# Gate and up projections that move the high and low halves of the activations in one matmul, with squares folded on VectorE and masks added in place

## What is computed

```python
x = x + 0.5 * swiglu(rmsnorm(x, g1), w_gate, w_up, w_down)      # F = 2816
h = rmsnorm(x, g_mix)
o = gla_attention(...)  or  mla_attention(...)                   # layer 0, layer 1
x = x + concat([o, memory_cross_attention(...)]) @ w_out
x = x + 0.5 * swiglu(rmsnorm(x, g2), w_gate2, w_up2, w_down2)

def swiglu(h, w_gate, w_up, w_down):
    return (silu(h @ w_gate) * (h @ w_up)) @ w_down
```

## Time and profile before

| | us |
|---|---|
| median of 3 executions (1849.73 to 1852.27) | 1849.98 |
| profiled execution, its own time | 1849.6 |
| its span in the profile | 1847.8 |
| TensorE busy | 1731.1 |
| VectorE busy | 1185.5 |
| ScalarE busy | 906.3 |
| GpSimd busy | 146.6 |
| DMA traffic, mean | 156 GB/s |
| granted TensorE clock, mean share of full speed | 0.971 |

### The profile page before, as it was taken

The page is one execution under the profiler, slowest core; times in us unless marked ns, Lnnn a source line. Parts: engine busy times, 40 slices in busy tenths (PEclk is TensorE's granted clock), DMA queues, the critical chain, the costliest instruction groups (busy, mean ns, idle before and its releaser), DMA issues.

```text
span 1847.8 us, 33177 instructions
## 1 busy us (share of the span) xinstructions
PE 1731.1 (94%) x12716; PEld 1619.7 (88%) x12716; DVE 1185.5 (64%) x1681; ACT 906.3 (49%) x1462; POOL 146.6 (8%) x125
## 2 busy tenths in 40 slices
PE   7999999899999999999799999997899988989997
PEld 7999987599999999987589999874899977689997
DVE  5756676456656676677656765657666568666554
ACT  5544453544444454445545544546554445655443
POOL 1100300001000200032102000300100003010000
PEclk9999999999999999999899999999899999999998
DMA  6555444245655465545134655440365544036552
GB/s 234 198 184 183 145 150 161 67 160 172 200 185 174 135 217 184 178 160 182 46 125 149 204 180 183 157 140 12 103 218 182 187 140 137 16 111 217 189 183 70
DMA packets 79333, 287.34 MB, mean 156 GB/s; under 512 B 8848, under 2 KB 9232, under 8 KB 79008
## 3 DMA queue, kind: packets, MB, share of 16 engines
q1 hardware_dynamic: 78336, 282.25, 46.0%
q0 software_dynamic: 608, 3.15, 0.5%
q10 hardware_dynamic: 320, 1.01, 0.2%
HBM read 285.31 MB, written 1.05 MB: 155 GB/s over the span
## 4 chain that ended last, share of the span: by engine, by line
PE 68%; issue 12%; DVE 10%; ACT 4%; POOL 3%; DMA 2%; POOLq 0%; ACTq 0%; SPq 0%; DVEq 0%
PE ps L1779 10%; PE ps L1780 10%; PE ps L1781 10%; PE ps L1718 8%; PE ps L1765 7%; PE ps L1767 7%; PE ps L1766 7%; DMA raw<-units 2%; POOL rows L570 2%; DVE act_lo L1098 2%; PE ps L2060 1%; DVE wlo L1064 1%; PE ps L2024 1%; DVE inv L1580 1%; ACT prob L1007 1%
## 5 line engine op out<-in xcount | busy, mean ns | idle before, releaser
L1239 DVE TENSOR_TENSOR wlo<-raw,whi 128x1024 fp32r<-128x1024 f32 x380 | 464.2, 1225 | 256.2 <-ACT whi L838 255.3
L1779 PE MATMUL ps<-act_hi,wlo 128*128 128x256 f32 x2016 | 575.2, 285 | 4.2 <-DVE prob L1247 4.2
L1781 PE MATMUL ps<-act_lo,whi 128*128 128x256 f32 x2016 | 573.3, 284 | 0.0
L1780 PE MATMUL ps<-act_hi,whi 128*128 128x256 f32 x2016 | 573.2, 284 | 0.0
L838 ACT ACTIVATE whi<-raw 128x1024 fp32r<-128x1024 f32 x380 | 397.8, 1049 | 169.4 <-PE ps L1781 120.9
L1779 PEld LDWEIGHTS ps<-act_hi,wlo 128*128 128x128 f32 x2016 | 390.0, 193 | 4.8 <-issue 4.6
L1780 PEld LDWEIGHTS ps<-act_hi,whi 128*128 128x128 f32 x2016 | 389.9, 193 | 0.2
L1781 PEld LDWEIGHTS ps<-act_lo,whi 128*128 128x128 f32 x2016 | 389.8, 193 | 0.0
L1765 PE MATMUL ps<-hid_hi,wlo 128*128 128x256 f32 x1056 | 298.8, 283 | 0.0
L1766 PE MATMUL ps<-hid_hi,whi 128*128 128x256 f32 x1056 | 298.8, 283 | 0.0
L1767 PE MATMUL ps<-hid_lo,whi 128*128 128x256 f32 x1056 | 298.8, 283 | 0.0
(11 more groups left out here) (208 smaller groups left out, 2123.9 us busy)
## 6 DMA issues: line engine op xcount, KB each, us to landing
raw<-units SPq DMA_DIRECT2D x534, 512.0 KB, 3.4
arena<-mem_in POOLq DMA_DIRECT2D x2, 1024.0 KB, 8.0
x<-x_in SPq DMA_DIRECT2D x4, 256.0 KB, 5.0
arena<-mem_in POOLq DMA_DIRECT2D x4, 256.0 KB, 4.6
out<-x SPq DMA_DIRECT2D x4, 256.0 KB, 2.3
const<-const_in ACTq DMA_DIRECT2D x1, 816.0 KB, 6.7
row<-row_in ACTq DMA_DIRECT2D x1, 134.0 KB, 6.6
gain<-gain_in SPq DMA_DIRECT2D x1, 76.5 KB, 2.0
```

Of the source, the lines that this page charges most:

```text
L1239: V.tensor_tensor(wlo[:, u % RING, :], raw[:, u % RAW, :], whi[:, u % RING, :].bitcast(F32), ALU.subtract).then_inc(lo_ready, 1)
L1779: T.matmul(out_, wlo[:, slot, w], act_hi[:, k, :], start=k == 0, stop=False)
L1780: T.matmul(out_, whi[:, slot, w], act_hi[:, k, :], start=False, stop=False)
L1781: ins = T.matmul(out_, whi[:, slot, w], act_lo[:, k, :], start=False, stop=k == KD - 1)
```

## The change

1. `act_hi` and `act_lo` become the two halves of one tile, `acts[:, k, 0]` and `acts[:, k, 1]`. In `columns`, `whi` is loaded once per k and moves both halves, 512 columns, into a whole bank; `wlo` moves the high half, 256 columns, into the bank's first half. Gate and up of a chunk lie in two banks (4 and 5, or 6 and 7), and chunks alternate between the pairs as before.
2. On evacuation ScalarE copies the two banks' second halves to SBUF (`lows_out`, a new instruction per chunk), VectorE adds the first halves (`added_up`, new), then multiplies by the inverse norm from SBUF to SBUF. gate(c) waits for `added_up` of chunk c-2. In the first chunk of a stage VectorE's mean, diagonal and copy of the spread now stand behind that add; before, they stood ahead of chunk 0 and waited for no chunk.
3. The four squares of x are folded on VectorE, right after the low parts of the activations and ahead of the next two unit splits. GpSimd keeps the folding of the memory tokens' squares.
4. The masks hold the 256 columns in which anything is masked, and are added in place in PSUM. For causal jobs the two token tiles' scores change places in the bank, so that those columns are contiguous. The wait for the transposes of job j-4 goes. The constants shrink from 1632 to 1120 columns beside the identity.
5. For sink heads the two small VectorE steps become one, with a negated sink prepared once, and ScalarE's two sink exponentials of a job become one.

The core of the diff:

```diff
+        acts = sb("acts", [P, 16, 2, S], F32R)
+        act_hi, act_lo = acts[:, :, 0, :], acts[:, :, 1, :]
...
@@ ScalarE, chunk
+                        act.wait_ge(unit_used, i * RING + (U0 + (2 * (c + 1) if c < 3 else 3 * c)))
+                        nc.scalar.activation(gate_up_rms[:, c % 2], ps[:, bank:bank + 2, S:2 * S], ACT.Copy
+                                             ).then_inc(lows_out, 1)
...
@@ VectorE, norm and norm_beside_memory
-                    self.squares += BANKS
+                    self.folded()
...
@@ VectorE, chunk
-                        V.tensor_tensor(gate_up_rms[:, c % 2], ps[:, bank, :].rearrange("p (e s) -> p e s", e=2),
-                                        doubled(inv_rms), ALU.mult).then_inc(scaled_ready, 1)
+                        dve.wait_ge(lows_out, i * 2 + n)
+                        V.tensor_tensor(both, ps[:, bank:bank + 2, 0:S], both, ALU.add).then_inc(added_up, 1)
+                        if c == 0:
+                            self.mean(name, 0)
...
+                            self.diagonal(name)
+                            self.spread(0)
+                            dve.wait_ge(inv_ready, self.spreads)
+                        dve.wait_ge(added_up, i * 2 + n)
+                        V.tensor_tensor(both, both, doubled(inv_rms), ALU.mult).then_inc(scaled_ready, 1)
...
@@ VectorE, attention
+                                middle = ps[:, j % NB, P:3 * P]
+                                self.step(V.tensor_tensor(middle, middle, job["mask"], ALU.add))
...
-                                self.step(V.tensor_scalar(inv[:, j % NB, :], inv[:, j % NB, :], HD ** -0.5, job["sink"],
-                                                          ALU.mult, ALU.max))
-                                V.tensor_scalar(top[:, j % NB, :], inv[:, j % NB, :], -1.0, None,
-                                                ALU.mult).then_inc(top_ready, 1)
+                                V.tensor_scalar(top[:, j % NB, :], inv[:, j % NB, :], -HD ** -0.5, job["minus_sink"],
+                                                ALU.mult, ALU.min).then_inc(top_ready, 1)
...
@@ TensorE, columns
-                            T.matmul(out_, wlo[:, slot, w], act_hi[:, k, :], start=k == 0, stop=False)
-                            T.matmul(out_, whi[:, slot, w], act_hi[:, k, :], start=False, stop=False)
-                            ins = T.matmul(out_, whi[:, slot, w], act_lo[:, k, :], start=False, stop=k == KD - 1)
+                            T.matmul(ps[:, bank, :], whi[:, slot, w], acts[:, k].rearrange("p e s -> p (e s)"),
+                                     start=k == 0, stop=False)
+                            ins = T.matmul(ps[:, bank, 0:S], wlo[:, slot, w], act_hi[:, k, :], start=False,
+                                           stop=k == KD - 1)
...
@@ TensorE, gate; the feed-forward stage's order
+                        if c >= 2:
+                            pe.wait_ge(added_up, i * 2 + (gu + c - 1))
...
-                    self.columns_of_fold(0, 5)
+                    self.columns_of_fold(0, 0)
...
-                    self.spread(5)
+                    self.spread(0)
...
+                    pe.wait_ge(inv_ready, self.diags)
                     down(0, 0, first=True)
-                    pe.wait_ge(inv_ready, self.diags)
```

More of the change, by code:

```diff
@@ L318, in build @@
         rstd = sb("rstd", [P, STAT_W])
+        minus_sink = sb("minus_sink", [P, QH])
         minus_half = sb("minus_half", [P, 32])
@@ L495, in keys_of, with scores_of @@
             return (t + 1) * P if job["causal"] else S
+        def scores_of(job, j, t):
+            at = S * (1 - t if job["causal"] else t)
+            return ps[:, j % NB, at:at + keys_of(job, t)]
         def queries_of(job, k):
@@ L1000, in attention @@
                                 n_keys = keys_of(job, t)
[L1001 to L1005 removed]
+                                if job["sink"] is not None and t == 0:
+                                    nc.scalar.activation(es[:, j % NB, :], top[:, j % NB, :], ACT.Exp, bias=job["sink"])
+                                src = scores_of(job, j, t)
                                 scale = HD ** -0.5 if job["rms"] is None else query_scale(job)[:, t:t + 1]
@@ L1100, in low, with folded @@
                                            ).then_inc(norm_lo, 1)
+                def folded(self):
+                    for b in range(1, BANKS):
+                        dve.wait_ge(square_ready, self.squares + b + 1)
+                        self.step(V.tensor_tensor(sq[:, 0], sq[:, 0], sq[:, b], ALU.add))
+                    self.squares += BANKS
+                    V.tensor_tensor(fold[:, 0, :], sq[:, 0, 0:S], sq[:, 0, S:2 * S], ALU.add).then_inc(fold_ready, 1)
                 def mean(self, name, bank):
@@ L1290, in end @@
                     if end.startswith(("post", "fpost")):
-                        for b in range(1, BANKS):
-                            dve.wait_ge(square_ready, self.squares + b + 1)
-                            self.step(V.tensor_tensor(sq[:, 0], sq[:, 0], sq[:, b], ALU.add))
-                        self.squares += BANKS
-                        V.tensor_tensor(fold[:, 0, :], sq[:, 0, 0:S], sq[:, 0, S:2 * S], ALU.add
-                                        ).then_inc(fold_ready, 1)
+                        self.folded()
                         self.mean(end, 5)
@@ L1320, in gla @@
                     dve.wait_ge(params_landed, 48)
+                    V.tensor_scalar(minus_sink[:], row[:, ROW_AT["sink"]:ROW_AT["sink"] + QH], -1.0, None, ALU.mult)
                     self.norm_memory_keys(0)
```

86 lines of the change are left out of this document (32 added, 54 removed).

## The result

The changed kernel takes **1819.1 us** in the median (1817.2 to 1820.5, four runs), the kernel before beside it 1850.4 (1849.7 to 1852.3): a ratio of 0.983, with a 95% interval of 0.982 to 0.985. It is 31 us faster where 37 were forecast, inside the range, 6 us short of the forecast. The profiled execution took 1819.4 us, its span 1817.6.

The account below looks back on a forecast made before the run. TensorE, busy 94% of the span, was taken as the bound in the gate and up projections. Terms of 21.5 + 8 + 1 + 0.5 + 6 = 37.0 us off 1849.6 gave 1812.6, forecast as a 1813 us median; range 1804 to 1830.

Parts of the forecast that it names:

- Two matmuls for three: Gate and up projections (`columns`): one matmul fewer per k saves 11 ns, 2016 times less the first stage's loss, 21.5 us.
- I take 0.349, nearer to the end whose sum is explained: In `columns`, a 512 and a 256 per k cost 0.349 us, chosen from 0.347 to 0.354.
- Rival (a): In `columns`, a 256 beside a 512 costs more on top, so a k saves perhaps 2.5 ns: 1829 us; 10%.
- rival (c): In `columns`, a 512 ahead of a shorter matmul costs 0.254, a k 0.374: slower, 1862 us; 3%.
- (d): In `columns`, TensorE takes the 512 as two parts, so the pair gains nothing: 1834 us; 2%.
- The longer evacuation: Feed-forward chunks: ScalarE's new copy and VectorE's new add are covered by TensorE's work; 0, up to 2 us of loss.
- The fold: Stage starts: folding on VectorE removes TensorE's waits for GpSimd, 8 us, plus 1 us in the last stage.
- three stages give 1.5 each: Starts of three feed-forward stages: the vanished wait and faster low parts gain 1.5 us each, 4.5 together.
- The fifth stage: nothing: Fifth stage's start: no gain from faster low parts, since TensorE itself is slow there at the lower clock.
- The first stage's start: First stage's loads: a later diagonal loses about 1 us, smaller constants save 1.6 us of traffic; 0.5 us gained.
- Masks and sinks: Attention: cheaper mask add and one small step fewer give 5.5 us in banded jobs, 0.5 in causal: 6 us.
- Rival (b): Fold, evacuation and masks: the small parts don't come, some 4 of 15.5 us stay: 1824 us; 20%.

Follow-up runs that it names:

- The later memory steps: The changed kernel with ScalarE's and VectorE's two memory-token steps placed later in three feed-forward stages: 1811.6 us, ratio 0.980 to the kernel before.

## Why the prediction was nearly right, point by point

**1. Two matmuls for three: mechanism right, term mis-sized.** 21.5 us forecast, 14 measured. The step that failed is "I take 0.349, nearer to the end whose sum is explained". The sum of rows 5 and 6 put a 512 and a 256 side by side at what each costs among its like. The unexplained 6 ns of the earlier trace rows were the warning: that pair, and not the 192 of the earlier trace rows, was the like of a 256 beside a 512. The bound of 0.354 held, to the nanosecond. In its place the runs showed an extra at the start of each run of 512s behind 256s, 7 ns a pair when they take turns. Rival (a) had the right cause and too low a size, rival (c)'s 0.254 behind a 512 was a third there: 0.236 for 0.227. For (d) nothing spoke. The Trainium skill's 2.5 ns per instruction ("TensorE: Matmul & The Clock Gate", section "Wait — 56ns, not 53.3ns?"), by estimate 4.9 us in all, are a third of what the instruction gave: the trace doesn't agree.

**2. The longer evacuation: right at the end of a stage, wrong beside the memory steps.** There is no wait ahead of down(21), as forecast. In the first stage ScalarE's copy of chunk 21 begins at 201.38, `hid_lo` ends at 206.42, 5.0 us later (5.2 forecast), and down(21) starts at 206.93:

```profile
201.38 0.60 ACT L853 ACTIVATE prob<-ps 128x512 f32<-128x512 f32 x1 [1.71 <-PE ps L1785]
```

```profile
206.00 0.42 DVE L1275 TENSOR_TENSOR hid_lo<-hid,hid_hi 128x256 fp32r<-128x256 f32 x1
```

But "VectorE then works 5.9 of about 8.4 us: covered" counted an ordinary chunk. At chunks 2 and 3 of three stages eight hi and eight low parts in all come on top, and in the first a DMA. The later memory steps gave back 5.6, 1.3 and 1.1 us. Not all of it was the change's doing: of the first stage's wait at most 1.5 are (5.05 for 3.5, but 3.9 when the changed kernel was repeated); the third stage was as long as the second to 0.1 us before, so its 1.3 are; the fourth was 0.9 longer before too.

**3. The fold: right in place, too small.** 9 us forecast; undoing it cost 13 outside the first stage and the first mixer, where the forecast had 7.8. No wait is left at `columns_of_fold` at the start of the feed-forward stages, no wait for the diagonal in the second, low parts at 0.41. The term that was mis-sized is "three stages give 1.5 each". What was left out is what the wait did to the clock: 1.4 of waiting was followed by 3 us at 0.50, so that the start cost 3.1, not 1.5. The prediction named this only in its last sentence and put no number on it, though the windows of before would have given one. "The fifth stage: nothing" was wrong as well: the first chunk there goes from 8.9 to 7.7 us, like the sixth's from 8.9 to 7.4, 2.8 for both instead of 1. Both first chunks were bound by the low parts, which GpSimd's adds had slowed: with the fold back on GpSimd both take 8.9 again. The clock, low at the start of the fifth stage's first chunk before and after, did not keep that gain away.

**4. The first stage's start.** 0.5 forecast. The stage gained nothing at all: 2.1 in `columns`, less 0.9 in the first chunk and 1.5 at the memory tokens; TensorE's wait for the fold, 0.8, became one of 1.0 for the diagonal. When the changed kernel was repeated, the first chunk and the memory tokens were a gain of 0.4 and a loss of 0.4, and the stage was 0.8 longer still, so nothing can be said of the constants.

**5. Masks and sinks: too large.** 6 forecast, 3.9 shown. A job went to 2.75, above the "right" of 2.6 to 2.7 and below the "wrong" of 2.9; the small step was priced from start to start without its follower, and the causal jobs gave nothing that shows. The 0.43 for the mask add came true partly by luck: the 0.43 of the earlier trace rows belongs to `hid_lo`, which is made from SBUF tiles alone, while the prediction took it for a step that reads PSUM.

**Not in the sum: the instruction packet.** The first mixer lost 3.1 us where 1.2 were forecast as gained. The packet's part in that is shown for the late load, 2 us, and not for the whole stage: padding it away made the stage only 0.8 to 2.8 us shorter than in the two executions of the changed kernel. No row of before showed it as a cost, but two facts stood there: a program that gets shorter, and a stage that follows its loads one by one.

Together: 14 + 13 + 3.9, less about 4 for the first stage and the memory steps and 4 for the first mixer, are 23; the two profiled executions lie 30 apart. Of the 7 left, 1.3 are the clock of the fourth stage (0.991 before, 1.00 with the fold back on GpSimd), 1 is the earlier start of the first mixer's chain, and some 3 lie in the second and third mixer, which vary by 0.8 and 1.3 between executions of one kernel. The rest, under 2, stays open. Rival (b), the small parts don't come, fell: the fold alone brought 13. Rival (c) fell: a pair never cost more than three.

## What to carry to other kernels

Price a mix of instruction sizes from a mix: the time from one start to the next depends on the neighbour, and here the unexplained excess in the nearest row was a better estimate than the explained sum from farther ones. Price a wait of TensorE with the stretch at half clock behind it, and ask of every cover whether it holds at the chunk with the most on top, not at the usual one. When one stage that an edit doesn't touch changes by 2 us or more, look at what its loads share the DMA with, the program's own code among it.

## What the runs showed of the hardware

- A 512-column and a 256-column fp32r matmul in turn take 0.236 and 0.118 us from start to start, 0.354 per pair; among their like 0.227 and 0.120. In the order 512, 256, 256, 512 a pair takes 0.350, in runs of eight 0.350, in runs of sixteen 0.349. The first five 512s of a run take 0.228 to 0.236, all later ones 0.227.
- A 512 KB weight load with a 16 KB packet of instructions beside it takes 4.4 to 5.7 us to land (ten profiles), without it 3.2 or 3.3 (four).
- VectorE's add with PSUM as input and output, 128x256, takes 0.43 us; its copy of 128x256 from PSUM to SBUF takes 0.42.
- Eight 128x256 low parts take 3.25 us alone and 4.30 or 5.32 while GpSimd adds.
- Behind a wait of 1.4 us TensorE's granted clock was 0.50 for 3 us at all three stage starts of the kernel before. Behind waits of 1.5 us with the fold back on GpSimd, it was so at two of three, and stayed at 1.00 at the third.
